# Dilated attention, value products: the values stationary for two heads at a time, the result turned back

## The reference

```python
qkv = proj[..., :n_qkv].reshape(B, S, 3, N_DIL_GROUPS * DIL_HEADS, HEAD_DIM)
q, k = rope(qkv[:, :, 0], pos), rope(qkv[:, :, 1], pos)
# for each group, queries t over keys t, t-d, ..., t-window
scores = einsum('bqhd,bkhd->bhqk', q, k) * HEAD_DIM ** -0.5     # masked
m = max(scores); p = exp(scores - m); den = sum(p)
out = einsum('bhqk,bkhd->bqhd', p, v) / den
lse = m + log(den)
# over the three groups: alpha = softmax(lse); o = sum(alpha * out)
y = (o * silu(gate)) @ w_out
```

## Time and profile before

| | |
|---|---|
| median of 3 runs | 2210.07 us (2203.17 to 2214.13) |
| the profiled execution | 2206.05 us, its span 2204.2 us |
| TensorE matmul busy | 2117.1 us, 96% of the span |
| VectorE, ScalarE, GpSimd busy | 967.0, 866.5, 840.0 us |
| attention of the first layer | about 96 to 575 us of the span |

### The profile page before, as it was taken

One profiled execution on the slowest core, in us unless ns is written; L12 is line 12 of the kernel. 1 busy time (PEld: TensorE's weight loads), 2 busy tenths in 40 slices (PEclk: granted clock), 3 DMA queues, 4 the chain that ended last, 5 costly groups with the idle time before them and its releaser, 6 DMA issues. The chain is left out here.

```text
span 2204.2 us, 26734 instructions
## 1 busy us (share of the span) xinstructions
PE 2117.1 (96%) x10366; PEld 1684.7 (76%) x10366; DVE 967.0 (44%) x1642; ACT 866.5 (39%) x1769; POOL 840.0 (38%) x447
## 2 busy tenths in 40 slices
PE   8999999999899999989999999999999899999998
PEld 6788888887658767678778888787774478888886
DVE  2444645444444575654571311258666532111211
ACT  4554556564344565543331232333322232221221
POOL 4433233332333323353444445344333152444442
PEclk9999999999999999999999999999999999999999
DMA  6313233232622212132433333233344242323321
GB/s 220 96 58 96 58 96 97 77 97 78 222 92 73 88 58 77 51 122 77 134 96 107 90 101 105 83 93 99 104 149 130 85 153 67 96 96 96 96 96 58
DMA packets 130204, 218.67 MB, mean 99 GB/s; under 512 B 8712, under 2 KB 58552, under 8 KB 129872
## 3 DMA queue, kind: packets, MB, share of 16 engines
q1 hardware_dynamic: 111152, 169.68, 25.3%
q0 software_dynamic: 8096, 28.93, 4.1%
q10 hardware_dynamic: 10832, 18.35, 2.4%
HBM read 198.29 MB, written 18.04 MB: 98 GB/s over the span
## 5 line engine op out<-in xcount | busy, mean ns | idle before, releaser
L2530 POOL TENSOR_TENSOR lo_ring<-raw_ring,hi_ring 128x1024 fp32r<-128x1024 f32 (+1 forms) x288 | 694.5, 2434 | 1009.2 <-ACT hi_ring L2173 1009.1
L1117 PE MATMUL bank<-xh,hi_ring 128*128 128x512 f32 (+1 forms) x1568 | 610.7, 389 | 3.6 <-DVE xl L1601 2.9
L1117 PE MATMUL bank<-xh,lo_ring 128*128 128x512 f32 (+1 forms) x1568 | 593.9, 379 | 0.0
L1117 PE MATMUL bank<-xl,hi_ring 128*128 128x512 f32 (+1 forms) x1568 | 592.6, 378 | 0.0
L2173 ACT CAST hi_ring<-raw_ring 128x1024 fp32r<-128x1024 f32 (+1 forms) x288 | 288.1, 1045 | 406.5 <-PE bank L1117 385.3
L1117 PEld LDWEIGHTS bank<-xh,hi_ring 128*128 128x128 f32 x1568 | 297.1, 189 | 66.2 <-issue 13.8
L1117 PEld LDWEIGHTS bank<-xh,lo_ring 128*128 128x128 f32 x1568 | 296.5, 189 | 56.4
L1117 PEld LDWEIGHTS bank<-xl,hi_ring 128*128 128x128 f32 x1568 | 297.2, 190 | 52.7 <-issue 2.2
L1117 PE MATMUL bank<-hi_ring,xh 128*128 128x512 f32 (+1 forms) x512 | 209.4, 409 | 9.7 <-DVE xl L1755 4.9
L1117 PE MATMUL bank<-hi_ring,xl 128*128 128x512 f32 (+1 forms) x512 | 201.5, 394 | 0.0
L1117 PE MATMUL bank<-lo_ring,xh 128*128 128x512 f32 (+1 forms) x512 | 201.2, 393 | 0.0
(11 more groups left out here) (289 smaller groups left out, 2675.2 us busy)
## 6 DMA issues: line engine op xcount, KB each, us to landing
raw_ring<-in_ffn_w_in SPq DMA_DIRECT2D x176, 256.0 KB, 3.1
raw_ring<-in_dil_w_in SPq DMA_DIRECT2D x80, 512.0 KB, 3.6
raw_ring<-in_ffn_w_out SPq DMA_DIRECT2D x44, 512.0 KB, 3.7
raw_ring<-in_diff_w_in SPq DMA_DIRECT2D x32, 512.0 KB, 3.7
raw_ring<-in_w_in SPq DMA_DIRECT2D x32, 512.0 KB, 3.6
arena<-scratch_heads POOLq DMA_DIRECT2D x4, 1584.0 KB, 12.0
scratch_gates<-arena ACTq DMA_DIRECT2D x24, 256.0 KB, 2.0
arena<-scratch_gates POOLq DMA_DIRECT2D x24, 256.0 KB, 5.0
```

The lines of the kernel that those rows point to most:

```text
L1117: ins = T.matmul(bank[pb][:, cols if p.form == "feature" else slice(0, p.cols)], lhsT, rhs, start=(k == 0 and m == 0 and half != 1), stop= ...
L2530: G.tensor_tensor(lo, raw_ring[:, p % RAW, 0:q.kq * q.n], hi.bitcast(F32), ALU.subtract).then_inc(lowered, 1)
```

## The change

The plan has one `d_values` job for a pair of heads instead of one for each head, and a new job `d_back` for each pair. In `d_values` the two heads' values are stationary, 64 columns each, and the turned probabilities move; head c's result goes to PSUM partitions 64c to 64c + 63 of bank 7, so that it is [two heads' dimensions] x [512 tokens]. ScalarE copies it to a new SBUF tile `d_out`. `d_back` transposes its four 128x128 tiles into bank 7 again, and VectorE copies the 512 columns to `stage`. In units 0 and 1 a pair's `d_values` stands at r == 0 two pairs on, in the others at r == 3 one pair on, where the even head's job was; `d_back` stands at r == 1. Units 0 and 1 have 22 slots instead of 21. `d_values` waits for the odd head's turned blocks. The store of a unit waits for the last `d_back`.

```diff
-        for slot in range(4 * 4 + (6 if g else 5)):
+        for slot in range(4 * 4 + 6):
             p, r = divmod(slot, 4)
             if r == 0:
                 if p >= 2 and g == 0:
-                    plan.job("d_values", u, 2 * p - 3, banks=(7,))
+                    plan.job("d_values", u, p - 2, banks=(7,))
...
             elif r == 1:
-                if p and g == 0:
+                if 1 <= p <= 4 and g == 0:
                     plan.job("d_rest", u, 2 * p - 2, banks=(6,))
...
-                if p >= 2 and g:
-                    plan.job("d_values", u, 2 * p - 3, banks=(7,))
+                if p >= 2:
+                    plan.job("d_back", u, p - 2, banks=(7,))
             elif r == 2:
...
                     plan.job("d_turn", u, 2 * p - 1, banks=(6,))
-                    if g == 0:
-                        plan.job("d_values", u, 2 * p - 2, banks=(7,))
             elif p and g == 0:
                 plan.job("d_rest", u, 2 * p - 1, banks=(6,))
             elif p:
-                plan.job("d_values", u, 2 * p - 2, banks=(7,))
+                plan.job("d_values", u, p - 1, banks=(7,))
...
+        d_out = carve(at, S)
...
-            def d_values(job, u, hh):
-                buf, s = u % 2, hh % 2
+            def d_values(job, u, p):
+                buf = u % 2
                 blocks = blocks_of[min(u // 2, 1)]
-                T.wait_ge(drained[6], use_of["d_rest" if u < 2 else "d_turn", job.n][0])
+                T.wait_ge(drained[6], use_of["d_rest" if u < 2 else "d_turn", 8 * u + 2 * p + 1][0])
                 empty(7, job.use[0])
                 for i in range(NT):
                     for m, (blk, kt) in enumerate(blocks[i]):
-                        ins = T.matmul(bank[7][:, i * HD:(i + 1) * HD], d_pt[:, s, blk, :], VV[:, buf, kt, hh * HD:(hh + 1) * HD],
-                                       start=(m == 0), stop=(m == len(blocks[i]) - 1))
+                        for c in range(2):
+                            hh = 2 * p + c
+                            ins = T.matmul(tile(bank[7][HD * c:HD * c + HD], i), VV[:, buf, kt, hh * HD:(hh + 1) * HD], d_pt[:, c, blk, :],
+                                           start=(m == 0), stop=(m == len(blocks[i]) - 1))
+                ins.then_inc(filled[7], 1)
+
+            def d_back(job, u, p):
+                empty(7, job.use[0])
+                for i in range(NT):
+                    ins = T.transpose(tile(bank[7], i), tile(d_out, i), ident)
                 ins.then_inc(filled[7], 1)
...
-                elif kind == "d_values":
-                    u, hh = a
+                elif kind == "d_back":
+                    u, p = a
                     V.wait_ge(filled[7], job.use[0])
-                    V.tensor_copy(stage[:, u % 2, :, hh, 0:HD], bank[7][:, 0:NT * HD].rearrange("p (a b) -> p a b", a=NT)).then_inc(drained[7], 1)
+                    V.tensor_copy(stage[:, u % 2, :, 2 * p:2 * p + 2, 0:HD],
+                                  bank[7][:, :].rearrange("p (i c d) -> p i c d", i=NT, c=2)).then_inc(drained[7], 1)
...
+                elif kind == "d_values":
+                    copy_out(7, job.use[0], d_out, bank[7][:, :])
...
-                G.wait_ge(drained[7], use_of["d_values", 8 * u + 7][0])
+                G.wait_ge(drained[7], use_of["d_back", 4 * u + 3][0])
```

More of the change, by code:

```diff
@@ L1442, in tensor_program @@
                     d_values(job, *a)
+                elif kind == "d_back":
+                    d_back(job, *a)
                 elif kind == "v_turn":
```

## The result

The changed kernel took 2226.92 us (median of 5 runs, 2220.34 to 2228.26); the kernel before took 2210.07. The ratio is 1.0075, 95% interval 1.0053 to 1.0096: **slower by 16.9 us**, where 10 were forecast. The profiled execution took 2228.26 us, its span 2226.5, 22.3 longer than that of before.

What follows compares the result with a forecast made beforehand. TensorE's queue was taken to bound the first layer's attention. Gains of 5.4 us against waits of 4.4 and 11.7 gave +10.7, rounded to +10, on the median 2210.07: 2220 us, range 2202 to 2233.

Steps and rivals of the forecast that it cites:

- The products: Value matmuls on TensorE: 0.75 us saved a pair in units 0 and 1, 0.15 in units 2 to 5.
- The copies: VectorE gives 48 copies (20.2 us) and gets 24 (16.5 us); ScalarE gets 24 (14.8 us), beside TensorE.
- The gain lost ahead of VectorE's copies: Second pairs of units 0 and 1: TensorE arrives 1.5 us sooner and waits longer, 3.0 us lost.
- The term: Net gain from the value matmuls in the attention: 6.0 - 3.0 + 2.4 = 5.4 us.
- ScalarE's copies at the ends of units 0 and 1: TensorE's d_back waits there for ScalarE's copy of bank 7, 2.2 us twice, 4.4 us.
- The waits in units 2 to 5: Values wait for VectorE's copy of the odd head's d_turn: 11.7 us in all.
- The choice to take units 3 and 4 at full size: Second pairs there: waits of 2.8 us each, recurring with GpSimd's lowering; by chance, 4.4 us less in total.
- The sum: Gains, ScalarE waits and VectorE waits over the first layer's attention: -5.4 + 4.4 + 11.7 = +10.7 us.
- The waits mostly don't come: Rival: TensorE's new waits stay mostly absent, faster or same, some 2190 to 2209 us; chance 0.20.
- ScalarE gets late: Rival: 24 copies delay ScalarE's casts to hi_ring, up to 14.8 us on top, 2228 to 2235; chance 0.17.
- The halves don't overlap: Rival: value matmuls on the two column halves run one by one, 26.4 us more, 2246; chance 0.05.
- down by some 8 us: Sign: TensorE's busy time in the layer falls by this much.

Runs made afterwards that it cites:

- second execution: The changed kernel measured and profiled once more, with no edit, beside the kernel before: 2226.41 us, ratio 1.0082.
- the spreading: Share of a unit's jobs over its products 0.93 instead of 0.88; alone on the kernel before: 2198.52 us, ratio 0.9952.
- the change spread further: The changed kernel with the share of a unit's jobs over its products 0.93 instead of 0.88: 2205.74 us, ratio 0.9993 to the kernel before.

## Why the prediction was right in its direction and short in its size

**The products: right.** Forecast 0.75 and 0.15 us saved a pair. From the starts of the products: in units 0 and 1 the vanished job gives 1.57, the wider one costs 0.31 more, the turning back 0.43: 0.83 saved. In units 2 to 5: -0.45 for the turning back in the place of a values job, +0.31: 0.14 saved. The copies came out as priced too: 24 of ScalarE's in 14.0 us (42.9 less 28.9; forecast 14.8), 24 of VectorE's in 16.4 (16.5). One reason given is not shown: that the load of 128 columns sets the old form's pace. With one half after the other the loads have 64 columns, and a record still takes 0.10 us beside the old form's 0.11.

**The gain lost ahead of VectorE's copies: half seen.** Forecast was 3.0 us at the second pairs of units 0 and 1, by TensorE arriving sooner at a wait. It measured 2.0 there. The same mechanism worked at a second kind of place that I did not look for, the last pair: the `d_turn` now reaches bank 6 before the `d_rest` copy has emptied it. TensorE in unit 0, second execution:
```profile
169.16 0.63 PE L1154 MATMUL bank<-consts,arena 128*128 128x128 f32 x4 [1.22 <-DVE arena L2061]
```
Two of them, 2.4 us. The term is 6.6 - 2.0 - 2.4 + 2.3 = 4.5 us gained, not 5.4.

**ScalarE's copies at the ends of units 0 and 1: right**, 2.09 and 2.08 us of wait for 2.2.

**The waits in units 2 to 5: right in place, order and nearly in size.** Unit 2's last pair 1.45 (forecast 1.1, a little more behind it), units 3 and 4 2.98 each (2.8), unit 5's two 4.6 and 1.7, and the two old ones of 0.56 gone: 5.2 net, and a small new one of 0.4 on top (forecast 5.0). VectorE and TensorE in unit 5, second execution, with the chain that the prediction took from the earlier trace rows: the copy stands behind a step that waits for ScalarE.
```profile
566.49 0.69 DVE L1539 SCALAR_TENSOR_TENSOR arena<-arena,bank 128x512 f32<-128x512 f32 x1 [3.72 <-ACT arena L2190]
567.10 0.68 DVE L2058 COPY arena<-bank 128x512 f32<-128x512 f32 x1
...
567.83 1.97 PE L1172 MATMUL bank<-arena 128*64 128x128 f32 x16 [4.64 <-DVE arena L2058]
```
The choice to take units 3 and 4 at full size, by the row and not by chance, was right: moving the lowering took both waits away.

**The step that failed: each wait was priced at its own length.** The sum had no term for the granted clock. It also rounded its own +10.7 down to +10. Of the second execution's 17.4 us, about 2.8 are half clock behind the ends of units 0 and 1 (1.4 each, by unit 1's shift of 1.0 without it) and about 2.0 in unit 5, what its waits and products leave of 7.0. The first has 4.3 more, in units 3 and 4. Where no half clock falls, the forecast holds: units 2, 3 and 4 shift by 0.8, 2.4 and 2.4 (0.5, 2.2, 2.2), unit 1 by 1.0 (0.7). Some 5 us of clock and 2 us of smaller gain and longer waits are the 17.4 less 10.7. Over all executions it is the same picture: 11.6 us more at full clock, near the sum's 10.7, and up to 6.5 more withheld. The Trainium skill (TensorE: Matmul & The Clock Gate, on how the gate bites in real kernels) warns of idle gaps of TensorE. The traces agree that the stretches stand behind waits, but not that a wait's length settles it: 2.98 us had one, 2.99 had none, and of two waits of 2.09 in one execution one had it. The length changes how often. Of TensorE's waits over 1 us between 95 and 600 us in all fourteen traces, none of the 70 of up to 1.74 us has half clock at it, 17 of the 36 of 1.80 to 2.99 us have, and all 12 of 3.90 us and more.

**The rivals.** "The waits mostly don't come" is excluded by the list of waits. "ScalarE gets late" as well: no wait of a product for `lo_ring` appears in the layer. "The halves don't overlap" by the 1.75 us, and by the 2.89 where they are made not to. One of my signs was poorly chosen: busy time "down by some 8 us" reads 19.7, because a fixed window holds less work once waits have pushed it out.

What stays open: why the kernel with the new form in units 0 and 1 alone is granted more clock behind the layer; why the layer of the kernel before gains 7.0 us by the spreading where its waits fall by 5.9; and what decides, for a wait of 1.8 to 3.0 us, whether half clock follows.

## What to carry to other kernels

Fewer matmuls on the bound engine are worth only what the next wait leaves: here 8.9 us of saved work met 22 us of new waits, since merging two heads into one job took the slack that the second head's job had. When a change adds waits of some 2 us and more to a TensorE that was hardly idle, price them at more than their length: the half clock behind them was worth another fifth to two fifths here (4.8 and 9.1 on 22 us in the two traces). And before a new job order is judged, try the one number that spreads the jobs, on both kernels: it was worth 9.4 us to the old one and, by the ratios, some 20 to the new, more than the change itself.

## What the runs showed that I had not expected

- Half clock behind waits as short as 1.8 us (once, in the change spread further) and 1.9 and 2.1 us, in places that change between executions of one kernel while the wait itself stays the same (2.98 and 2.99). In unit 3 it took the price from 2.4 to 5.2 us.
- Two accumulations in one bank, on the two halves of the columns in turn, run at 0.06 us a record (28 in 1.68); the same 28 with one half after the other take 0.10 a record.
- A rotary add of 128x512 took 1.11 us without GpSimd's lowering beside it and 3.06 to 3.18 with it, and the long one moved when the lowering was moved.
